# A two-layer hybrid decoder step on one Trainium2 core: index dots issued in pairs, a selection that finds the dropped keys, and a later chain for the sample attention

## The reference, cut to what matters

```python
def indexer_scores(qi, wi, ki):
    dots = einsum('bqhd,bsd->bqhs', qi, ki) * (D_IDX ** -0.5)      # 8 index heads of 32
    w = wi * (N_IDX_HEADS ** -0.5)
    return einsum('bqh,bqhs->bqs', w, relu(dots))

# prompt: for each query the 132 best of the admissible keys
sc = where(key_pos <= q_pos, indexer_scores(qi, wi, ki), -inf)
_, idx = lax.top_k(sc, 132)          # ties go to the lower index
# softmax attention over the chosen keys only; the samples choose 64 of their 257
```

## Time and profile before

| | |
|---|---|
| median of 3 runs | 852.49 us (852.21 to 853.35) |
| profiled execution | 854.95 us |
| its span, first to last instruction | 853.6 us |
| PE busy | 783.3 us (92%) |
| DVE busy | 611.2 us (72%) |
| ACT, POOL busy | 328.5 us (38%), 332.2 us (39%) |
| mean granted clock of TensorE | 0.950 |
| moved by DMA | 75.08 MB, 88 GB/s |

### The profile page before, as it was taken

One profiled execution on the slowest core, in us unless ns is written; L12 is line 12 of the kernel. 1 busy time (PEld: TensorE's weight loads), 2 busy tenths in 40 slices (PEclk: granted clock), 3 DMA queues, 4 the chain that ended last, 5 costly groups with the idle time before them and its releaser, 6 DMA issues. The chain is left out here.

```text
span 853.6 us, 13008 instructions
## 1 busy us (share of the span) xinstructions
PE 783.3 (92%) x4476; PEld 610.1 (71%) x4476; DVE 611.2 (72%) x1434; ACT 328.5 (38%) x830; POOL 332.2 (39%) x318
## 2 busy tenths in 40 slices
PE   4898989999888899999998899899998898999998
PEld 4895645558777786777998655355887786777888
DVE  3547898899998986435543879989999899632222
ACT  3724344435844232224132443354464633322202
POOL 0033876952753730011110558788254465000000
PEclk9999998999988999999999999799998899899999
DMA  4533040124141545014034303103231356400312
GB/s 171 157 103 102 4 135 14 46 71 136 53 105 60 159 153 198 1 50 139 2 102 116 103 1 106 45 2 101 91 114 46 72 153 207 148 0 4 103 44 101
DMA packets 57282, 75.08 MB, mean 88 GB/s; under 512 B 13233, under 2 KB 32889, under 8 KB 57185
## 3 DMA queue, kind: packets, MB, share of 16 engines
q1 hardware_dynamic: 57106, 74.18, 28.7%
q10 hardware_dynamic: 111, 0.08, 0.0%
HBM read 67.27 MB, written 7.61 MB: 88 GB/s over the span
## 5 line engine op out<-in xcount | busy, mean ns | idle before, releaser
L1175 PE MATMUL R<-x_hi,W_r 128*128 128x268 f32 x448 | 142.0, 317 | 26.4 <-DVE yT L1694 7.2
L1159 PE MATMUL R<-W_r,x_hi 128*128 128x512 f32 (+3 forms) x320 | 127.9, 400 | 12.3 <-DVE W_r L1500 12.3
L1177 PE MATMUL R<-x_hi,W_r 128*128 128x268 f32 x448 | 136.9, 306 | 0.0
L1176 PE MATMUL R<-x_lo,W_r 128*128 128x268 f32 x448 | 136.6, 305 | 0.0
L1188 PE MATMUL R<-yT,W 128*128 128x268 f32 (+2 forms) x768 | 129.2, 326 | 2.9 <-DVE yT L1500 2.9
L1188 PEld LDWEIGHTS R<-yT,W 128*128 128x128 f32 x768 | 111.2, 197 | 20.6 <-issue 7.8
L1160 PE MATMUL R<-W_r,x_hi 128*128 128x512 f32 (+3 forms) x320 | 121.0, 378 | 0.0
L1161 PE MATMUL R<-W_r,x_lo 128*128 128x512 f32 (+3 forms) x320 | 120.6, 377 | 0.0
L1175 PEld LDWEIGHTS R<-x_hi,W_r 128*128 128x128 f32 x448 | 93.1, 208 | 37.9 <-DVE yT L1694 11.2
L1500 DVE SCALAR_TENSOR_TENSOR cc<-uext,params,cc 128x528 f32<-128x528 f32 x120 | 112.5, 983 | 0.0
L773 POOL TENSOR_TENSOR W_r<-W,W_r 128x1024 fp32r<-128x1024 f32 x28 | 66.4, 2382 | 88.5 <-ACT W_r L891 88.3
(11 more groups left out here) (237 smaller groups left out, 1361.9 us busy)
## 6 DMA issues: line engine op xcount, KB each, us to landing
W<-in_w_in SPq DMA_DIRECT2D x52, 512.0 KB, 4.1
KV<-in_cache_k SPq DMA_DIRECT2D x32, 256.0 KB, 2.9
W<-in_w_out SPq DMA_DIRECT2D x8, 1024.0 KB, 7.3
KV<-in_cache_v SPq DMA_DIRECT2D x32, 256.0 KB, 4.0
ubx<-qkv_rows SPq DMA_DIRECT2D x16, 256.0 KB, 3.6
zi<-z_rows SPq DMA_DIRECT2D x16, 196.0 KB, 3.6
W<-in_w_in SPq DMA_DIRECT2D x8, 296.0 KB, 3.3
out_new_k_prompt<-kz SPq DMA_DIRECT2D x8, 256.0 KB, 2.0
```

Of the source, the lines that this page charges most:

```text
L1159: pe.matmul(out, x_hi[:, kc, rows], hi, start=(kc == 0), stop=False)
L1175: pe.matmul(out, hi[:, cols], x_hi[:, kc, toks], start=(kc == 0), stop=False)
L1176: pe.matmul(out, hi[:, cols], x_lo[:, kc, toks], start=False, stop=False)
L1177: m = pe.matmul(out, lo[:, cols], x_hi[:, kc, toks], start=False, stop=(kc == KC - 1))
```

## The change

1. **Dots in pairs.** PIECES is reordered so that two heads of the same tile and key range follow each other, and dots(first) issues both behind every fourth chunk. The pair waits until ACT has read all pieces before it.
2. **Selection.** Tile 1 looks for the 12 keys that it drops: its scores are negated into a field in reversed order (LOW, in the unused end of its row of bias), two rounds mark 12 keys and 4 sentinels, and the mask is read back. select(i) does one step of a tile (a maximum, a replacement, or a mask), and each tile waits for its own last step alone. No round is left in the q projections. Before unit 0 there are all 7 steps of tile 1, 30 steps of tile 2 and 28 of tile 3; units 0 to 3 have the rest of these and, like the units up to 22 that NO_ROUND leaves, two steps of tile 4.
3. **Sample attention.** Page steps in units 22 to 29, index 30, selection 32 to 35, logits 36, exp 37, norm 38, turn 39, keep 40, page products 41, 42, 43, 44, their masking 43 and 45, the sum behind PE's loop, the gate in DVE's unit 45.
4. **The queue.** w_load(30) and (31) are issued in step b = 2 of the page loop, (32) and (33) behind the loop as before.

```diff
@@ constants
+LOW = SENT + WIDTH[1] + 12
+LOW_ROUNDS = (WIDTH[1] - TOPK_P + SENT) // 8
-PIECES = [(i, h, a, b) for pair in ((1, 2), (3, 4)) for h in range(IH) for i in pair
-          for a, b in ([(0, WIDTH[i])] if WIDTH[i] <= 512 else [(0, WIDTH[i] // 2), (WIDTH[i] // 2, WIDTH[i])])]
+PIECES = [(i, h, a, b) for pair in ((1, 2), (3, 4)) for two in range(0, IH, 2) for i in pair
+          for a, b in ([(0, WIDTH[i])] if WIDTH[i] <= 512 else [(0, WIDTH[i] // 2), (WIDTH[i] // 2, WIDTH[i])])
+          for h in (two, two + 1)]
-NO_ROUND = (7, 9, 10, 12, 16, 18, 20)
-ROUNDS_EARLY = 3
+NO_ROUND = (9, 10, 12, 16, 18)
+EARLY_STEPS, EARLY_REST = 28, 5
-PV_STEPS, PV_KEEP, PV_SUM = (37, 39, 41, 43), (40, 43), 44
-SX = {... "pages": 18, "swish": 20, "index": 26,
-      "index_turn": 27, "topk": 28, "logits": 32, "exp": 33, "norm": 34, "turn": 35, "keep": 36, "pv": 37, "ahead": 41, "gate": 44}
+PV_STEPS, PV_KEEP, PV_SUM = (41, 42, 43, 44), (43, 45), 45
+SX = {... "pages": 22, "swish": 20, "index": 30,
+      "index_turn": 31, "topk": 32, "logits": 36, "exp": 37, "norm": 38, "turn": 39, "keep": 40, "pv": 41, "ahead": 41, "gate": 45}
@@ sync_layer, the page loop
-            for m in range(30, 34):
-                w_load(m)
+                if b == 2:
+                    w_load(30)
+                    w_load(31)
+            w_load(32)
+            w_load(33)
@@ pool_layer
             misc0.did(pool.memset(bias[:, :, 0:SENT], BIG))
+            misc0.did(pool.memset(bias[:, 0, LOW:LOW + SENT], BIG))
@@ unit_tm
-                    if first_dots is not None and kc % 2:
-                        dots(first_dots + kc // 2)
+                    if first_dots is not None and kc % 4 == 3:
+                        dots(first_dots + kc // 4 * 2)
@@ tensor_layer
-            def dots(p):
-                i, h, lo, hi = PIECES[p]
-                if p == 0:
-                    pe.wait_ge(*idxk_s.at(NT))
-                if p >= 2:
-                    pe.wait_ge(*rel_s.at(p - 1))
+            def dots(first):
+                if first == 0:
+                    pe.wait_ge(*idxk_s.at(NT))
+                else:
+                    pe.wait_ge(*rel_s.at(first))
+                for p in (first, first + 1):
+                    i, h, lo, hi = PIECES[p]
...
+            weigh_pages_sum()
             pe.wait_ge(*y_s.at(3))
             pe.wait_ge(*ys_s.at(1))
@@ vector_layer
+            steps_of, mark, slot_of = {1: 0, 2: 0, 3: 0, 4: 0}, {}, {1: 3, 2: 0, 3: 1, 4: 2}
+            low = bias[:, 0, LOW:LOW + SENT + WIDTH[1]]
+            flipped = bias[:, 0, LOW + SENT + WIDTH[1] - 1:LOW + SENT - 1:-1]
+
+            def select(i):
+                k, best = steps_of[i], m8[0:ROWS[i], slot_of[i], :]
+                field, n = (low, LOW_ROUNDS) if i == 1 else (area(i), ROUNDS)
+                k -= i == 1
+                if k > 2 * n + 1:
+                    return
+                if i in mark:
+                    dve.wait_ge(*tk_s.at(mark[i]))
+                if k < 0:
+                    tk_s.did(dve.tensor_scalar(flipped, area(1, SENT), -1.0, None, ALU.mult))
+                elif k == 2 * n:
+                    if i == 1:
+                        tk_s.did(dve.tensor_scalar(area(1, SENT), flipped, CUT, NEG, ALU.is_lt, ALU.mult))
+                    else:
+                        tk_s.did(dve.tensor_scalar(area(i), area(i), CUT, NEG, ALU.is_gt, ALU.mult))
+                elif k == 2 * n + 1:
+                    causal(i, tk_s)
+                elif k % 2 == 0:
+                    tk_s.did(dve.max(best, field))
+                else:
+                    tk_s.did(dve.match_replace(field, best, field, GONE))
+                steps_of[i] += 1
+                mark[i] = tk_s.n
+
+            def late(n):
+                if n < EARLY_REST:
+                    select(2)
+                    select(3)
+                if n not in NO_ROUND:
+                    select(4)
+                    if n < EARLY_REST:
+                        select(2)
+                        select(3)
+                    select(4)
@@ vector_layer, q projections and before unit 0
                 kq_sum(NT + i)
-                if i < 4:
-                    topk_round((1, 2))
             rest(18)
             rest(19)
-            topk_round((1, 2))
...
-            for _ in range(NT + 2, ROUNDS):
-                topk_round((1, 2))
-            to_bias((1, 2))
...
+            for _ in range(EARLY_STEPS):
+                select(1)
+                select(2)
+                select(3)
...
-            for _ in range(ROUNDS_EARLY):
-                more_topk(0)
@@ vector_layer, the loop over units
-                more_topk(n)
-                if n == 22:
-                    assert rounds[0] == ROUNDS
-                    to_bias((3, 4))
-                    tb34 = tk_s.n
+                late(n)
```

More of the change, by code:

```diff
@@ L147 @@
 TAPS_IDX, TAPS_K, TAPS_Q = 8, (3, 3, 3, 3, 3), (2, 2, 2, 1, 1)
-NO_ROUND = (7, 9, 10, 12, 16, 18, 20)
-ROUNDS_EARLY = 3
+NO_ROUND = (9, 10, 12, 16, 18)
+EARLY_STEPS, EARLY_REST = 28, 5
 CONV_END, PD_END, LN_END = 2 * CONV_W + 6, 14, 7
 SD = {"isc": 3, "logit_in": 29, "negmax": 31, "etp": 34}
-PV_STEPS, PV_KEEP, PV_SUM = (37, 39, 41, 43), (40, 43), 44
-SX = {"pool_diff": 9, "pool_diff2": 10, "ln_diag": 12, "ln_mul": 16, "ln_tanh": 17, "pages": 18, "swish": 20, "index": 26,
-      "index_turn": 27, "topk": 28, "logits": 32, "exp": 33, "norm": 34, "turn": 35, "keep": 36, "pv": 37, "ahead": 41, "gate": 44}
+PV_STEPS, PV_KEEP, PV_SUM = (41, 42, 43, 44), (43, 45), 45
+SX = {"pool_diff": 9, "pool_diff2": 10, "ln_diag": 12, "ln_mul": 16, "ln_tanh": 17, "pages": 22, "swish": 20, "index": 30,
+      "index_turn": 31, "topk": 32, "logits": 36, "exp": 37, "norm": 38, "turn": 39, "keep": 40, "pv": 41, "ahead": 41, "gate": 45}
 def constants():
@@ L269, in program @@
         gt = sb("gt", 128, 2, HALF)
-        small = sb("small", 128, 192)
+        small = sb("small", 128, 216)
         kic = sb("kic", 128, N_SAMPLE, N_PAGES, ID)
@@ L309, in program @@
         krn = small[:, 58:74].rearrange("p (a b) -> p a b", a=2)
-        m8 = small[:, 74:90].rearrange("p (a b) -> p a b", a=2)
+        m8 = small[:, 182:214].rearrange("p (a b) -> p a b", a=4)
         lnv = small[:, 90:98]
@@ L1261, in kq_turn @@
                 kqt_s.did(m)
-            def dots(p):
-                i, h, lo, hi = PIECES[p]
-                if p == 0:
+            def dots(first):
+                if first == 0:
                     pe.wait_ge(*idxk_s.at(NT))
-                if p >= 2:
-                    pe.wait_ge(*rel_s.at(p - 1))
-                b = 32 * (h % 4)
-                ix_s.did(pe.matmul(A[0:ROWS[i], p % 2, 0:hi - lo], qkT[b:b + 32, h // 4, START[i]:START[i] + ROWS[i]],
-                                   qkT[b:b + 32, 2, lo:hi], start=True, stop=True))
+                else:
+                    pe.wait_ge(*rel_s.at(first))
+                for p in (first, first + 1):
+                    i, h, lo, hi = PIECES[p]
+                    b = 32 * (h % 4)
+                    ix_s.did(pe.matmul(A[0:ROWS[i], p % 2, 0:hi - lo], qkT[b:b + 32, h // 4, START[i]:START[i] + ROWS[i]],
+                                       qkT[b:b + 32, 2, lo:hi], start=True, stop=True))
             p = 0
@@ L1528, in vector_layer @@
             dve.wait_ge(*st_t.at(2))
-            dve.wait_ge(*misc0.at(3))
+            dve.wait_ge(*misc0.at(4))
             def tok(h):
@@ L1571, in causal @@
                 s.did(dve.tensor_tensor(d, d, tri[0:ROWS[i], 0:ROWS[i]], ALU.add))
-            def topk_round(pair):
-                for x, i in enumerate(pair):
-                    dve.wait_ge(*tk_s.at(tk_s.n - 1)) if tk_s.n > 1 else None
-                    tk_s.did(dve.max(m8[0:ROWS[i], x, :], area(i)))
-                for x, i in enumerate(pair):
-                    dve.wait_ge(*tk_s.at(tk_s.n - 1))
-                    tk_s.did(dve.match_replace(area(i), m8[0:ROWS[i], x, :], area(i), GONE))
@@ L1582, in to_bias @@
-            def to_bias(pair):
-                for i in pair:
-                    dve.wait_ge(*tk_s.at(tk_s.n))
-                    tk_s.did(dve.tensor_scalar(area(i), area(i), CUT, NEG, ALU.is_gt, ALU.mult))
-                for i in pair:
-                    dve.wait_ge(*tk_s.at(tk_s.n))
-                    causal(i, tk_s)
+            steps_of, mark, slot_of = {1: 0, 2: 0, 3: 0, 4: 0}, {}, {1: 3, 2: 0, 3: 1, 4: 2}
+            low = bias[:, 0, LOW:LOW + SENT + WIDTH[1]]
+            flipped = bias[:, 0, LOW + SENT + WIDTH[1] - 1:LOW + SENT - 1:-1]
@@ L1673, in vector_layer @@
                 conv_s.did(dve.tensor_scalar(cc[:, c, NTOK:TOK], wsum[:, c, :], prm[:, 10 + c:11 + c], None, ALU.add))
-            for _ in range(NT + 2, ROUNDS):
-                topk_round((1, 2))
-            to_bias((1, 2))
-            tb12 = tk_s.n
-            rounds = [0]
-            def more_topk(n):
-                if rounds[0] < ROUNDS and n not in NO_ROUND:
-                    topk_round((3, 4))
```

(10 more changed lines are left out.)

## The result

The kernel after takes **863.9 us** in the median (859.8 to 865.9) where before takes 852.4: a ratio of **1.0132** (95% interval 1.0088 to 1.0177), slower by 1.3%. The profiled execution took 865.85 us with a span of 864.5, at a mean granted clock of 0.935 (before: 854.95, 853.6 and 0.950). Each ratio in this text counts fast executions alone: of the twelve of e9 the five at 859 us and more are left out, and its trace is of one of these (859.8).

The account below looks back on a forecast made before the run. PE was taken as the engine of the span, with DVE setting its pace in the middle of each layer. Terms summed to -4.9 us a layer, -9.8 for two: 842.7 us against the median, range 830 to 853.

Parts of the forecast that it names:

- Weights ahead of the spreads: Loads of w_out, 2 MB, before row spreads and key pages: nothing; as a rival +3 us a layer, 849, chance 0.08.
- Tail: Units 41 to 44 and the layer's end: page waits, probabilities' copy, moved sum and low clock, +7.5 us a layer.
- The three waits: Units 41 to 44: PE waits three times for value pages, about 1.5 us each, +4.5 (0 to 6).
- The sum behind the loop: Layer's end: sums move behind DVE's last masking, and the slow clock falls on the third output part, +0.8 us.
- q stage: q projections: pairs save PE 9.0 us, four selection rounds leave DVE; -7.5 us a layer (bounds -5.0 and -10).
- my lower bound: q projections: at least -5.0 us a layer from the four selection rounds taken off DVE alone.
- Pairs side by side: Dots of q and k projections: the second lies beside the first, so a pair costs one; 9.0 us of PE in q.
- the rival: Pairs cost three halves or run in series: 2.5 to 5 of q's 9.0 us lost, 848 to 853, chance 0.11.
- Block before item 0: Between q and item 0: DVE's selection work goes from 26.0 to 28.0 us, +2.0 a layer.
- Units 0 to 8: Eight rounds, 18.6 us of DVE, become rests of tiles 2 and 3 and nine of tile 4: -1.0 a layer.
- Page steps, units 18 to 24: Units 18 to 21 lose four page steps, units 26 to 29 gain four: -6.5 us a layer (0 to -8).
- The slower rival: Units 41 to 44: three waits put PE on the low clock, tail from 12.4 us a layer, 859, chance 0.10.

Follow-up runs that it names:

- e9: Kernel before with the new selections alone (single dots, chain in its old place): ratio 0.9992; median 855.1 us of all twelve executions, 847.1 of the seven counted.
- e1: Kernel after with output weight loads 30 and 31 put back behind the page loop: 850.7 us, ratio 1.0019 to before.
- e7: Kernel after with weight loads 30 and 31 issued by ScalarE at unit 25 instead of SyncE's queue: 864.6 us, ratio 1.0164 to before.
- e8: Kernel after with only load 30 ahead of the spreads and load 31 behind the page loop: 855.4 us, ratio 1.0062 to before.
- e12: As e1, but only the first four value pages are fetched and all four sets of products use them: 841.8 us, ratio 0.9889 to before.
- e6: As e5, but the sum of page products and the second masking stand behind the loop: 841.0 us, ratio 0.9899 to before.
- e4: Kernel before with the 40 dots a layer issued as 20 pairs and nothing else: 849.6 us, ratio 0.9995.
- e11: As e5, but both dots of a pair lie on the same 32 rows (heads h and h + 4): 836.0 us, ratio 0.9809 to before.
- e10: As e5, with tile 4's selection from unit 5 and the rests of tiles 2 and 3 over eight units: 834.3 us, ratio 0.9803 to before.
- e2: Kernel after with sample chain, sum and output weight loads in their old place; pairs and selections stay: 843.2 us, ratio 0.9912 to before.
- e5: As e1, with sample selection in two units and softmax steps closer, so value page products, sum and gate stand as before: 834.7 us, ratio 0.9815.

## Why the prediction was wrong

I forecast 842.7 with faster at 0.82; it came out at 863.9, outside the range. The body of the layer, up to item 26, came out at -10.9 and -9.3 where I had -13.0. Two prices behind it were wrong, and both point the same way.

- **Weights ahead of the spreads: "nothing, and 3 us if they don't".** This is the step that failed. Measured 4.8 us a layer by the times (after against e1), 5.6 and 6.1 in the trace. I asked when 2 MB would be through (6 us, two units) and not who else wanted the DMA engines: each page step moves 1 MB too (two pages, two spreads). The moved steps now meet the weights from unit 25 on, and the steps stand in a chain (row, POOL, DVE, PE), so a row that POOL misses in unit 27 stops PE in unit 29. e1, e7 and e8 show it: the loss goes with the loads, is the same on another queue, and 3.7 of its 9.6 us with one load. As a rival it had 3 us and a chance of 0.08.
- **Tail: +7.5 forecast, +9.9 and +9.5 measured.** Mechanism right, sizes off. The three waits: 4.5 forecast, 2.3 + 1.9 + 2.1 = 6.3 in the rows of layer 1, 5.5 a layer by e12. The sum behind the loop: 0.8 forecast, 3.5 by e6. Its place was well reckoned (0.5 later); what I took from before is the slow clock's price, 1.7, and on the third part with its transposes it is 1.9 + 0.9. The 1.6 for low clock behind the waits doesn't show: the output units behind them take 3.87, as in e12.
- **q stage: -7.5 forecast, -6.6 and -7.4 measured** (175.33 to 168.78; in layer 1 588.42 to 585.61, from a start that is 4.6 later). Right, but my lower bound ("-5.0, the rounds alone") was false: selections alone bring 0.2 there. With PE busy 46.3 of 47 us, and still 46.2 in e9, nothing taken off DVE could show until PE's own work shrank. The two must go together, as e4 and e9 show.
- **Pairs side by side:** right (0.94 us). By the rule that I had set against it (the Trainium skill, TensorE: Matmul & The Clock Gate, Part 3: Packing small matmuls) a pair would be three halves, some 1.3 to 1.4 us; the pairs of the trace after take 0.94. The price I gave the rival didn't follow either: with ten pairs in the q stage a third half of 0.44 is 4.4 us a layer and 8.7 in all, not "some 5". And e11 shows that even 1.61 changes the time by less than the runs can tell, so this rival should have had hardly any price.
- **Block before item 0: +2.0 forecast,** +0.9 measured (-6.6 to -5.7), and +0.8 in layer 1.
- **Units 0 to 8: -1.0 forecast,** +2.0 measured (item 0 to 9: -5.7 to -3.7, and the same in layer 1). The rests of tiles 2 and 3 and the start of tile 4 make units 0 to 2 take 3.5 to 5.1 us where they took 2.8, and the long mask stands in unit 2. e10 takes this loss away and gets nothing for it.
- **Page steps, units 18 to 24: -6.5 forecast,** -7.2 and -4.8 measured between items 9 and 26. Not all of it is the steps' own: e2, where they stay, gains 2.9 and 1.1 in the same stretch. e5 against e2 (0.9815 and 0.9912) gives the moved steps with the shorter chain 8 us, 4.1 a layer. That the number came out near is in part luck.
- **The slower rival** named the tail alone and asked for 12.4 us a layer. The tail brought 9.7, the spreads 5 more: two cases that I had counted as exclusive came together. With them the sum is -4.9 + 9.7 - 7.5 + 5 = +2.3 a layer, where the trace has +4.6 and +6.3. Of the 2 to 4 us still lacking, units 0 to 8 are 3 (above); the rest is the smaller gain of layer 1, which I can only book from the trace.

That e5 differs from e1 by the tail alone isn't fully shown: its chain is also shorter. e12 and e6 reach the same 9 us from the other side (5.5 + 3.5).

## What to carry to other kernels

A step moved in time takes its DMAs along: before a large load is placed ahead of it, add up what all steps of that stretch ask of the DMA engines, on every queue, and follow the chain that hangs on the smallest of these transfers. Where two engines are both full, price edits together and not one by one: each alone was worth nothing that could be told here, both together 7.5 us. And when a chain is started later, look for slack inside it (here two units of selection and two of softmax), so that its end, beside short units and a single set of buffers, can stay where it was.

## What was not expected of the hardware

- Products that wait for their operands show as long matmuls: in layer 1 steps of 2.9 to 3.3 us with 0 to 0.55 us of idle time shown, where the same step with its pages at hand takes 1.0.
- Two dots of 32 rows take 0.94 us on different rows of the array and 1.61 on the same rows (400 columns); 0.71 and 1.15 with 264. One alone takes 0.93: on the same rows, two cost 1.7 times one.
- A mask of DVE that starts while POOL's instruction runs ended 0.2 us behind that instruction, whatever its size. The mask of 276 columns started at 209.14 and ended at 211.38, POOL's split at 211.22; that of 404 columns ran from 214.26 to 215.12, POOL's next split to 214.90. With no instruction of POOL under way at their start, 532 columns took 0.43 us, and in e10 the 276 columns 0.29. That POOL holds the mask up fits all four; no run changed POOL's work alone.
